# Row combination of a pair moved behind the next pair's second gate-up, with two row buffers, the overflow test ahead of the last down, and another order at the end

## What is computed

```python
gates = jnp.sum(jax.nn.one_hot(expert_id, N_EXPERTS) * w_top[..., None], axis=1)   # 2 of 32 per token
for e in range(N_EXPERTS):
    a = jax.nn.silu(hf @ w_gate[e]) * (hf @ w_up[e])        # 2048 -> 512
    y = y + gates[:, e:e + 1] * (a @ w_down[e])             # 512 -> 2048
x = x + y
y_out = rmsnorm(x, g_final)
```

## Time and profile before

| | us |
|---|---|
| median of 3 runs | 1328.08 (1326.4 to 1328.87) |
| the profiled execution: its time | 1329.0 |
| its span | 1326.6 |
| TensorE busy | 1266.0 (95%) |
| VectorE, ScalarE, GpSimd busy | 464.2, 136.1, 114.6 |
| HBM read and written | 467.16 MB, 6.38 MB |

### The profile page before, as it was taken

The page is one execution under the profiler, slowest core; times in us unless marked ns, Lnnn a source line. Parts: engine busy times, 40 slices in busy tenths (PEclk is TensorE's granted clock), DMA queues, the critical chain, the costliest instruction groups (busy, mean ns, idle before and its releaser), DMA issues.

```text
span 1326.6 us, 14718 instructions
## 1 busy us (share of the span) xinstructions
PE 1266.0 (95%) x5793; PEld 637.9 (48%) x5793; DVE 464.2 (35%) x960; ACT 136.1 (10%) x281; POOL 114.6 (9%) x144
## 2 busy tenths in 40 slices
PE   8999999999999999999899989999999999999995
PEld 6777777777755333343333334333333334333331
DVE  6599984000342422323222222313222222312224
ACT  2100014000312000000000000000000000000003
POOL 6111394000000000000000000000000000000000
PEclk9999999999999999999999999999999999999998
DMA  9344434764599899999999999999999999999993
GB/s 285 136 129 152 149 109 141 253 253 159 207 370 408 346 421 428 428 426 429 428 430 427 434 426 435 424 429 429 429 429 429 434 427 427 429 428 430 422 424 129
DMA packets 74732, 461.95 MB, mean 348 GB/s; under 512 B 5231, under 2 KB 47343, under 8 KB 49059
## 3 DMA queue, kind: packets, MB, share of 16 engines
q1 hardware_dynamic: 71328, 453.00, 83.3%
q0 software_dynamic: 2800, 6.94, 1.7%
q10 hardware_dynamic: 571, 1.53, 0.3%
HBM read 467.16 MB, written 6.38 MB: 357 GB/s over the span
## 4 chain that ended last, share of the span: by engine, by line
PE 78%; DMA 17%; DVE 2%; ACT 1%; issue 1%; POOL 0%; DVEq 0%
PE bank L858 28%; PE bank L637 21%; DMA arena<-in_w_up_dram 16%; PE bank L944 11%; PE bank L836 9%; PE bank L832 2%; PE bank L820 2%; PE bank L716 1%; PE bank L840 1%; DMA arena<-in_state_pool_dram 1%; ACT aT L1146 1%; PE bank L708 0%; PE bank L935 0%; PE bank L734 0%; DVE arena L1487 0%
## 5 line engine op out<-in xcount | busy, mean ns | idle before, releaser
L858 PE MATMUL bank<-arena,xT 128*64 128x512 f32 x2040 | 451.0, 600 | 16.8 <-DMA arena<-in_w_up_dram 16.8
L858 PEld LDWEIGHTS bank<-arena,xT 128*64 128x64 f32 x2040 | 155.1, 138 | 307.5 <-issue 283.8
L637 PE MATMUL bank<-arena 128*128 128x288 f32 x1152 | 282.7, 407 | 0.0
L637 PEld LDWEIGHTS bank<-arena 128*128 128x128 f32 x1152 | 218.6, 190 | 63.0 <-issue 3.2
L944 PE MATMUL bank<-arena,aT 128*64 128x512 f32 x1024 | 226.8, 595 | 17.2 <-ACT aT L1146 17.2
L1521 DVE TENSOR_TENSOR a_sb<-sl_sb,bank 128x256 f32<-128x256 f32 x32 | 19.5, 610 | 383.2 <-ACT sl_sb L1144 383.2
L944 PEld LDWEIGHTS bank<-arena,aT 128*64 128x64 f32 x1024 | 74.1, 137 | 149.3 <-issue 135.2
L1538 DVE COPY ysb<-bank 64x512 f32<-64x512 f32 x64 | 44.1, 689 | 248.2 <-PE bank L944 247.7
L836 PE MATMUL bank<-ysb,wr 128*128 128x512 f32 x256 | 122.5, 617 | 2.5 <-issue 2.5
L1255 DVE SCALAR_TENSOR_TENSOR arena<-arena,wdw 128x256 f32<-128x256 f32 x240 | 104.4, 510 | 0.1
L1510 DVE TENSOR_TENSOR x1r<-x1r,bank 128x512 f32<-128x512 f32 x120 | 82.5, 687 | 31.5 <-PE bank L836 31.5
(11 more groups left out here) (275 smaller groups left out, 551.6 us busy)
## 6 DMA issues: line engine op xcount, KB each, us to landing
arena<-in_w_down_dram SPq DMA_DIRECT2D x27, 4096.0 KB, 27.6
arena<-in_w_up_dram SPq DMA_DIRECT2D x41, 2048.0 KB, 18.3
arena<-in_w_gate_dram SPq DMA_DIRECT2D x19, 4096.0 KB, 21.2
arena<-in_w_gate_dram SPq DMA_DIRECT2D x16, 2048.0 KB, 20.1
arena<-in_w_up_dram SPq DMA_DIRECT2D x7, 4096.0 KB, 24.8
arena<-in_w_in_dram SPq DMA_DIRECT2D x11, 2048.0 KB, 8.1
arena<-in_w_gate_dram SPq DMA_DIRECT2D x19, 1024.0 KB, 8.7
arena<-in_w_out_dram SPq DMA_DIRECT2D x8, 2048.0 KB, 8.7
```

Source lines behind the costliest of these rows:

```text
L637: last = pe.matmul(ps[bank][:, 0:NTOK], wsl[a][:, k, cc * P:(cc + 1) * P], rhs[:, k, :], start=(n == 0), stop=(n == KT - 1))
L858: mm = pe.matmul(ps[4 + s][BLK * h:BLK * (h + 1), :], xgT[:, k, BLK * s:BLK * (s + 1)], w[:, :, 256 * h:256 * (h + 1)], start=(k == 0), st ...
```

## The change

- The combination of pair i - 1 moves in pair i from behind the gate-up of s = 0 to behind the gate-up of s = 1. In the last pair (15) the sample and the first four products stay behind the gate-up of s = 0, in banks 3 and 2, and the other four come after its down, in banks 0 and 1.
- Two row buffers (`yrows`, the second in a part of `x1r` that is free by then) and two tables (`to_token`) take turns. The sample's product uses bank 3, so the second product already waits for its addition. ScalarE's and VectorE's loops hold two pairs an iteration for that.
- The last down stands behind the overflow test, in `last_down`; its first bank's end releases ScalarE, its second's VectorE.
- At the end the sample is combined first, then the first 128 tokens, the sum over the sample's parts, and the second 128. GpSimd multiplies the second half of the second 128 tokens' rows by `g_final`, ScalarE scales them by the root and sends them; VectorE's half goes by SyncE.

```diff
-LASTB = ((0, 1, 7, 4), (5, 6, 2, 3))
+LASTB = ((0, 1, 7, 5), (6, 2, 3, 0))
+SAMPLEB = 4
...
+        scaled = words(arena, SLOT + 2 * D + QC, 2 * QC)
...
-        yrows = ysb[:, :, :].rearrange("p s f -> p (s f)")
+        yrows = [ysb[:, :, :].rearrange("p s f -> p (s f)"), x1r[:, 1, :]]
...
-        to_token = words(wr, 0, NTOK)
+        to_token = [words(wr, a * NTOK, NTOK) for a in range(2)]
...
-                sp.wait_ge(out_ready, 2 * c + 2)
+                sp.wait_ge(out_ready, 2 + 3 * c)
                 sp.dma_start(y_prompt[0, 0:P, c * (D // 2):(c + 1) * (D // 2)], fin_rows[0][:, c * (D // 2):(c + 1) * (D // 2)]).then_inc(fin_out, 16)
             sample_rows = y_sample.rearrange("b t d -> (b t) d")
-            sp.wait_ge(out_ready, 5)
             for q in range(4):
                 sp.dma_start(sample_rows[:, q * QC:(q + 1) * QC], fin_q[NS * q:NS * (q + 1), :]).then_inc(fin_out, 16)
+            sp.wait_ge(out_ready, 7)
+            sp.dma_start(y_prompt[0, P:SEQ, 0:D // 2], fin_rows[1][:, 0:D // 2]).then_inc(fin_out, 16)
...
-            def combine_pair(i):
+            def combine_first(i, a, rows):
 
                 pe.wait_ge(to_token_ready, i + 1)
-                pe.wait_ge(y0_ready, 2 * i + 2)
-                pe.wait_ge(y1_ready, 2 * i + 2)
-                combine_sample(5).then_inc(comb_mm, 1)
-                for n in range(8):
-                    if n >= 2:
+                pe.wait_ge(y0_ready, rows)
+                pe.wait_ge(y1_ready, rows)
+                combine_sample(a, 3).then_inc(comb_mm, 1)
+                for n in range(4):
+                    if n >= 1:
                         pe.wait_ge(comb_added, 9 * i + n)
-                    combine(n // 4, n % 4, 2 + n % 2).then_inc(comb_mm, 1)
+                    combine(a, 0, n, 2 + n % 2).then_inc(comb_mm, 1)
+
+            def combine_second(i, a, banks):
+                for n in range(4):
+                    pe.wait_ge(comb_added, 9 * i + n + 4)
+                    combine(a, 1, n, banks[n % 2]).then_inc(comb_mm, 1)
...
+            def last_down():
+                for q in range(4):
+                    if q % 2 == 0:
+                        pe.wait_ge(half31_in[q // 2], 16)
+                    for col in range(2):
+                        mm = down(3, q, col)
+                        if q == 3:
+                            mm.then_inc(down_end, 1)
+
+            def pair(i, m0, rounds=None, first=False, ahead=True, last=False, over=None, open_end=False):
+
+                a = (m0 // 2) % 2
...
-                    if s == 0 and not first:
-                        combine_pair(i - 1)
+                    if s == 0 and last:
+                        combine_first(i - 1, 1 - a, 2 * i)
+                    if s == 1 and not first and over is None and not last:
+                        combine_first(i - 1, 1 - a, 2 * i + 1)
+                        combine_second(i - 1, 1 - a, (2, 3))
...
-                    if s == 0 and not first:
-                        pe.wait_ge(comb_added, 9 * i)
...
+                    if not first and not (last and s == 1):
+                        pe.wait_ge(comb_added, 9 * i if over is not None or s == 1 else 9 * i - 4 if last else 9 * i - 9)
+
+                    if s == 1 and (last or open_end):
+                        break
+                    for q in range(4):
+                        if over is None and rounds is None:
+                            early_down(n, q)
+                        elif over is None and q == 0:
+                            ring_down(m, rounds)
+                        down(m, q, 0)
+                        down(m, q, 1).then_inc(wd_used, 1)
+                    if last:
+                        combine_second(i - 1, 1 - a, (0, 1))
...
             pair(PAIRS - 1, 2, rounds=ROUNDS, ahead=False, last=True)
             with pe.If(n_over > 0):
-                with pe.Fori(0, OVP) as j:
+                for q in range(4):
+                    if q % 2 == 0:
+                        pe.wait_ge(half31_in[q // 2], 16)
+                    down(3, q, 0)
+                    down(3, q, 1).then_inc(wd_used, 1)
...
+            last_down()
 
             pe.wait_ge(to_token_ready, PAIRS)
-            pe.wait_ge(y0_ready, NE)
-            pe.wait_ge(y1_ready, NE)
-            for t in range(2):
-                for c in range(4):
-                    combine(t, c, LASTB[t][c]).then_inc(last_down, 1)
-            pe.wait_ge(last_added, 1)
-            combine_sample(LASTB[0][0]).then_inc(last_down, 1)
+            pe.wait_ge(y_last[0], 1)
+            pe.wait_ge(y_last[1], 1)
+            combine_sample(1, SAMPLEB).then_inc(last_mm, 1)
+            for c in range(4):
+                combine(1, 0, c, LASTB[0][c]).then_inc(last_mm, 1)
             pe.wait_ge(token_ready, 1)
             pe.wait_ge(squared2, 1)
-            pe.wait_ge(last_added, 2)
-            pe.matmul(ps[1][:, 0:TT], same_token[:, :], ssb[:, :], start=True, stop=True).then_inc(total_mm, 1)
+            pe.wait_ge(last_added, 1)
+            pe.matmul(ps[SAMPLEB][:, 0:TT], same_token[:, :], ssb[:, :], start=True, stop=True).then_inc(total_mm, 1)
+            for c in range(4):
+                if c == 3:
+                    pe.wait_ge(last_added, 2)
+                combine(1, 1, c, LASTB[1][c]).then_inc(last_mm, 1)
...
+            act.wait_ge(down_end, 1)
+            rows_out(1, 1, 0)
+            rows_out(1, 1, 1).then_inc(y_last[0], 1)
...
+            root(0, 0, 2)
+            for c in range(4):
                 square(1, c)
-            act.wait_ge(last_added, 9)
-            act.activation(squares_q, x1q[:, :], ACT.Square, accum_out=ssb[:, 2:3]).then_inc(squared2, 1)
-            root(1, 1, 3)
+            root(1, 2, 3)
+            act.wait_ge(last_root, 1)
             for c in range(2):
-                act.wait_ge(out_ready, 7 + 2 * c)
-                act.dma_start(y_prompt[0, P:SEQ, c * (D // 2):(c + 1) * (D // 2)],
-                              fin_rows[1][:, c * (D // 2):(c + 1) * (D // 2)]).then_inc(fin_out, 16)
+                act.wait_ge(scaled_ready, c + 1)
+                ins = act.activation(fin_rows[1][:, (2 + c) * QC:(3 + c) * QC], scaled[:, c * QC:(c + 1) * QC], ACT.Copy, scale=rs[:, 2:3])
+                ins.then_inc(act_scaled, 1)
+            act.wait_ge(act_scaled, 2)
+            act.dma_start(y_prompt[0, P:SEQ, D // 2:D], fin_rows[1][:, D // 2:D]).then_inc(fin_out, 16)
...
+            def add_second(i, banks):
+                for n in range(4):
+                    dve.wait_ge(comb_mm, 9 * i + n + 6)
+                    part = acc_rows[1][:, n * QC:(n + 1) * QC]
+                    dve.tensor_tensor(part, part, ps[banks[n % 2]][:, :], ALU.add).then_inc(comb_added, 1)
...
-                    if s == 0 and not first:
-                        add_combined(i - 1)
+                    if not first and not over:
+                        if s == 1 or last:
+                            if s == 0 or not last:
+                                add_first(i - 1)
+                            if not last:
+                                add_second(i - 1, (2, 3))
...
+                    if last:
+                        add_second(i - 1, (0, 1))
...
+            dve.wait_ge(last_mm, 1)
+            dve.tensor_tensor(x1q[:, :], x1q[:, :], ps[SAMPLEB][:, :], ALU.add).then_inc(last_added, 1)
             for c in range(4):
                 add_last(0, c)
             add_last(1, 0)
+            dve.wait_ge(total_mm, 1)
+            link(dve.tensor_scalar(va[:, 1:2], ps[SAMPLEB][:, 2:3], 1.0 / D, EPS, ALU.mult, ALU.add))
             mean_square(0).then_inc(act_in, 1)
             add_last(1, 1)
-            inverse_root(0, 0, 1)
+            inverse_root(0, 0, 2)
             dve.wait_ge(gfin_in, 16 * 5)
+            gain(0, 0)
+            add_last(1, 2)
+            gain(0, 1)
+            add_last(1, 3)
+            dve.scalar_tensor_tensor(out=fin_q, in0=x1q[:, :], scalar=rs[:, 1:2], in1=gfq,
+                                     op0=ALU.mult, op1=ALU.mult).then_inc(out_ready, 1)
+            gain(0, 2)
+            mean_square(1).then_inc(act_in, 1)
+            gain(0, 3)
+            inverse_root(1, 2, 3)
+            dve.sem_inc(last_root, 1)
...
+            pool.wait_ge(gfin_in, 16 * 5)
+            for c in range(2):
+                pool.wait_ge(last_added, 8 + c)
+                part = slice((2 + c) * QC, (3 + c) * QC)
+                pool.tensor_tensor(scaled[:, c * QC:(c + 1) * QC], acc_rows[1][:, part], gfin[:, part], ALU.mult).then_inc(scaled_ready, 1)
```

More of the change, by code:

```diff
@@ L892, in ring_down, with down @@
                 pe.wait_ge(ring_in[r], 16 * (ROUND_FILLS[r] * rounds + DOWN_FILL[m] + EARLY_FILLS[r]))
-            def pair(i, m0, rounds=None, first=False, ahead=True, last=False, over=None):
+            def down(m, q, col):
+                half, j = q // 2, q % 2
+                for h in range(2):
+                    mm = pe.matmul(ps[2 + col][BLK * h:BLK * (h + 1), :],
```

(35 more changed lines are left out.)

137 lines of the change are left out of this document (56 added, 81 removed).

## The result

The changed kernel takes 1335.92 us (median of 5 runs, 1333.88 to 1337.5); the kernel before took 1328.87 beside it. The ratio is 1.0055, 95% interval [1.0039, 1.0071]: slower by 0.55%. 1332.1 was forecast, with 1325.8 to 1335.5. The direction was right; the loss is 7.1 us where 4.0 was forecast. The profiled execution of the changed kernel took 1335.7, its span is 1333.7; before, the span was 1326.6. So 7.1 us have to be found between the two traces.

The account below looks back on a forecast made before the run. The middle was taken as bound by the weight transfer rate, the last stretch by TensorE and VectorE. -5.0 + 5.8 + 0.4 + 1.5 - 0.5 + 0.8 + 1.0 = +4.0 us on 1328.08 gave 1332.1, range 1325.8 to 1335.5.

Parts of the forecast that it names:

- The hole and its cause: Weight stream, pair 1: gate of expert 4 waits for expert 2's down, queue runs dry; closing it gives -5.0 us.
- The small hole near 487: Next lead load (up of expert 5) still issued at 487.49, meeting a nearly dry queue; 1.3 us lost again.
- The meeting point: Later pairs: the weight wait moves from the pair's head to the second gate-up; pair 15 starts +5.8 us later.
- Rival A: Second gate-up's weights are there in time, so 5.8 us aren't paid: 1326.3, or 1324.8 with the jump hidden; chance 0.20.
- Pair 15: Last pair's split combination: the third product after down 30 waits for VectorE's copies and addition, +0.4 us.
- The overflow test: Ahead of the last down: TensorE's jump over the overflow code is bare, +1.5 us (0 to 2.5).
- Rival C: Lower TensorE clock after the last weight wait, at gate-up 29: +1.7 us, 1333.8; chance 0.10.
- The reordered end: After the last down: -0.5 us for the order, +0.8 for halves sent at once, +1.0 for GpSimd beside VectorE.
- meetings of GpSimd and VectorE: At the end, GpSimd's two products hold up VectorE's gains with two SBUF operands, +1.0 us (0 to 2.5).
- B: Small prices at the end are nothing: code fetched ahead, or no GpSimd-VectorE meeting; 1329.8 to 1330.6; chance 0.26.
- D: The hole stays open as something besides the down holds expert 4's lead load; +5.0, 1337.1; chance 0.04.

Follow-up runs that it names:

- E7: As E5 (two buffers, test and end of the kernel before), but every combination early, behind the first gate-up; 1326.14 us, 0.9988 of the kernel before.
- E6: Against E7, only pair 1 combines late, all other pairs early; two buffers, test and end of before; 1322.93 us, 0.9962 of the kernel before.
- E5: Changed kernel with only the combination's move and two buffers kept, test and end as in the kernel before; 1326.13 us, 0.9988 of the kernel before.
- E2: Changed kernel without TensorE's overflow test and the overflow code behind it; 1330.05 us, 1.001 of the kernel before.
- E3: Changed kernel with the overflow test kept ahead of the last down, but the body jumped over cut to one wait; 1330.14 us, 1.0012 of the kernel before.
- E4: Changed kernel without GpSimd's products and ScalarE's scaling at the end, VectorE making all gains; 1333.78 us, 1.0052 of the kernel before.
- E1: Changed kernel with the overflow test put back behind the last down, combination and end as changed; 1329.04 us, 1.0003 of the kernel before.
- E8: E6 (only pair 1 late) with the changed kernel's order of the end; 1325.5 us, 0.9977 of the kernel before.

## Why the prediction was right or wrong, step by step

- **The hole and its cause: right.** Closed in the changed kernel, back in E7, passed on to the next lead load in E6. The stream came out 4.6 to 5.6 us ahead, for -5.0. The small hole near 487 is there too: the lead load is issued at 486.52 (487.49 before), and 488 to 490 runs at 0.74.
- **The meeting point: right, and shown.** 33.1 us lie between gate-up 29 and pair 15 (1250.95 - 1217.84), 33.2 were forecast, where 27.4 lay between the landing of gate 29 and pair 15 before. The waits moved to the second gate-up (four of the eleven are shorter than the 2 to 3 us named). The net of both, +0.8 in the sum, came to +0.16 between the two traces, which is less than the start of pair 15 varies from trace to trace. E5 against E7 (0.0 us) and E6 (3.2 us better than either) show it from the other side: the stream's gain is real, and the move in the later pairs is what gives it back. Rival A is out.
- **Pair 15: right.** +0.56 for +0.4, with a wait of 0.29 us at the third product.
- **The overflow test: the failed step.** Its place and kind were right, and E2 and E3 show the mechanism (the fetch of code that lies far away, not the test). The size was not: +1.5 stood in the sum, +4.5 came. Two terms of it. First the bare jump. I took the packet's length of 1.2 us for its price, and 2.46, the gap behind the down, as the upper bound. The packet's length is not the stall: from the packet to the first record it is 2.65 us here and 2.5 in E4, and 1.1 us come before it. And the packet of the earlier trace rows was not the start of the jump: q8's first one comes 3.4 us ahead of the down's end, so in the kernel before the fetch began beside the down's matmuls, and most of its price was in no gap. A gap in which part of the cost is hidden is no upper bound for it. Bare, it came to 3.67 us, of which 0.88 come back behind the down. Second the clock: the 4.13 us of idle time are followed by a down at 0.81, which costs 1.69 us. Rival C had that price, read from the same kind of row, but attached to the wait for gate 29 alone. The forecast gap itself, 2.0 us with its 0.46, was near the waits of 2.08 and 2.29 us, of which the second was followed by the lower clock, so the case belonged to it as well. With 3.67 - 0.88 + 1.69 in place of 1.5 the sum would have been +7.0.
- **The reordered end: right in kind, a little short.** +1.9 for +1.3 by the spans. The meetings of GpSimd and VectorE cost 1.4 us (forecast 1.0). VectorE's last gain ends at 16.76, by the forecast 15.8 + 1.0 = 16.8; that the sum for the gain's end came out is partly luck, as the meetings took 0.4 more and the rest 0.4 less. What lies behind it is the term that was short: 5.2 us for 3.7, so +1.5 for +0.8. The two halves leave at once, and SyncE's, issued at 1328.88, takes 4.1 us to land; its queue was issuing the sample rows until 1328.83, 0.35 us past the last gain's end, which the sum does not have. The medians of E1 against E5 put the whole end at 2.9 us, their ratios at 2.0; the difference is left open.
- **Rivals.** B (both small prices nothing) is out by E1 and E4. C's price was paid, at the last down instead of at gate-up 29; E8 shows it in the place where I had looked for it. D is out. B's range also had a slip: without the meetings alone the sum gives 1331.1, not 1330.6.
- **Left open.** Why the first product follows the packet behind the last down 0.9 us sooner in E5 and E7 than in the kernel before, and why 0.9 us less of their time lies outside the span; together that is their lead of 2 us. And of the 2.65 us from the packet on, only 1.22 are the packet's; what the rest is, no row names.

## What to carry to other kernels

A transfer that is started earlier helps only if the engine can use the data at the place where it waits: before a step is moved, work out the spacing at which the engine asks for each piece and compare it with the spacing of the stream. Where moving a step in the steady loop only shifts the wait, move it in the first rounds alone, where it opens the queue; here the move in all pairs was worth nothing, in the first pair 3.2 us, and in the first three 4.7 us (E7's 1326.14 against 1321.4; the latter from another group of runs, by the ratios it is 4.4). A jump over much code belongs where the engine waits for others anyway, and idle time of some us, put ahead of a stretch of matmuls on the path that sets the end, is to be priced twice, as the gap and as a slower stretch that may follow.

## What the runs showed of the hardware

**A jump over a large body cost TensorE 3.67 us where nothing covered it, a jump over one wait 0.25 us.** Behind the last down the long jump cost nothing in E1: its first packet came 3.4 us ahead of the down's end, and behind that VectorE's copies took 1.4 us. The stall and q8's packets, which E2 and E3 lack, agree with what the Trainium skill says of a taken branch out of the pages at hand (Runtime: NRT & Kernel Launch, section Instruction fetch mechanics); the price is this case's.

**The clock after a short idle time.** After 4.13 and 3.92 us of idle time the last down took 8.78 us (granted clock 0.81) and 9.26 us (0.76) instead of 7.09, so part of it ran at 1.2 instead of 2.4 GHz. After 0.46 and 0.71 us it took 7.09, in the eight other kernels of the study and in the one before. After waits of 2.0 to 2.9 us a gate-up takes 15.65 us in some cases and 13.95 in others, as in E8 at 1189.96 against 1194.16 in the earlier trace rows.

**GpSimd beside VectorE.** A gain of VectorE with both operands in SBUF took 0.75 us alone and 1.16 and 1.75 beside GpSimd's products, which took 1.65 each (3.30 for two) instead of 1.28. The one addition from PSUM wholly beside them, at 1321.89, took 0.68 us as elsewhere. That agrees with the Trainium skill (SBUF — State Buffer, section SBUF: two separate sides), by which a GpSimd operation that reads SBUF and a VectorE operation with two SBUF inputs hold each other up, and whichever starts first goes through.
